# One core, a chunked scan beside dense products: the decay arguments and the causal mask move from ScalarE's bias and GpSimd to VectorE, and a group's two squares are added before the product that makes their mean

## What is computed

```python
# 32 heads of 64 channels in 8 groups of 4 heads; B, C: 128 states for each group; 256 tokens
a = dt * A                                   # per token and head, negative
cum = jnp.cumsum(a, axis=1)
decay = jnp.exp(jnp.where(causal, cum[i] - cum[j], -jnp.inf))      # for each head
cb = jnp.einsum('bign,bjgn->bgij', C, B)                           # for each group
y = jnp.einsum('bgij,bghij,bjghp->bighp', cb, decay, x * dt)
y = y + x * d_skip
g = y * silu(z)                                                    # gated
g = g * lax.rsqrt(jnp.mean(jnp.square(g), axis=-1) + EPS)          # over the 256 channels of a group
y_b = g * norm_w
mixed = sigmoid(gate_a) * (y_a @ w_branch_gm) + sigmoid(gate_b) * (y_b @ w_branch_ssm)
```

## Time and profile before

| what | value |
|---|---|
| three executions | 1598.72, 1596.85, 1600.15 us (median 1598.72) |
| the profiled execution, its own time | 1598.4 us |
| its span, first to last instruction | 1596.6 us |
| mean granted TensorE clock | 0.988 of 2.4 GHz |
| busy: TensorE, weight loads, VectorE, ScalarE, GpSimd | 97%, 94%, 62%, 49%, 12% of the span |
| scan, 237.5 to 375 us: busy TensorE, VectorE, ScalarE, GpSimd | 110.45, 64.69, 69.93, 68.48 us of 137.5 |

### The profile page before, as it was taken

One profiled execution on the slowest core, in us unless ns is written; L12 is line 12 of the kernel. 1 busy time (PEld: TensorE's weight loads), 2 busy tenths in 40 slices (PEclk: granted clock), 3 DMA queues, 4 the chain that ended last, 5 costly groups with the idle time before them and its releaser, 6 DMA issues.

```text
span 1596.6 us, 30154 instructions
## 1 busy us (share of the span) xinstructions
PE 1541.6 (97%) x12471; PEld 1501.9 (94%) x12471; DVE 994.3 (62%) x1275; ACT 775.5 (49%) x1021; POOL 198.5 (12%) x186
## 2 busy tenths in 40 slices
PE   7999997879999999999999999999999999999997
PEld 5999997768999999999999899999999999899997
DVE  5887994445676555655465775555755558765545
ACT  3555565554465534544354554443544435554433
POOL 0300004553100010000012011001300013030001
PEclk9999999989999999999999999999999999999999
DMA  8976864433545544555545335555455553455550
GB/s 317 370 286 230 293 237 155 155 119 127 210 166 184 185 170 173 185 184 184 185 147 197 132 110 208 184 184 185 158 185 184 184 185 133 159 185 184 184 185 27
DMA packets 43497, 296.00 MB, mean 185 GB/s; under 512 B 5147, under 2 KB 7323, under 8 KB 8844
## 3 DMA queue, kind: packets, MB, share of 16 engines
q1 hardware_dynamic: 41244, 284.44, 49.3%
q0 software_dynamic: 2160, 10.22, 1.8%
HBM read 291.44 MB, written 3.19 MB: 185 GB/s over the span
## 4 chain that ended last, share of the span: by engine, by line
PE 87%; DVE 7%; ACT 3%; issue 1%; DMA 1%; POOL 0%; ACTq 0%; SPq 0%; DVEq 0%; POOLq 0%
PE banks L654 20%; PE banks L657 20%; PE banks L656 20%; PE banks L782 6%; PE banks L785 6%; PE banks L784 6%; DVE w_lo L1676 2%; ACT w_hi L1215 1%; DVE XS L1824 1%; PE banks L671 1%; PE banks L666 1%; PE banks L668 1%; DVE H L1832 1%; DMA rows<-cum_rows 1%; PE banks L813 0%
## 5 line engine op out<-in xcount | busy, mean ns | idle before, releaser
L1676 DVE TENSOR_TENSOR w_lo<-raw,w_hi 128x1024 fp32r<-128x1024 f32 x490 | 620.5, 1275 | 478.0 <-ACT w_hi L1215 472.8
L1215 ACT ACTIVATE w_hi<-raw 128x1024 fp32r<-128x1024 f32 x490 | 515.3, 1057 | 563.4 <-PE banks L657 405.1
L654 PE MATMUL banks<-H,w_lo 128*128 128x256 f32 x1696 | 477.7, 282 | 2.9 <-DVE w_lo L1676 1.9
L656 PE MATMUL banks<-H,w_hi 128*128 128x256 f32 x1696 | 477.2, 281 | 0.0
L657 PE MATMUL banks<-H,w_hi 128*128 128x256 f32 x1696 | 477.2, 281 | 0.0
L654 PEld LDWEIGHTS banks<-H,w_lo 128*128 128x128 f32 x1696 | 319.2, 188 | 3.7 <-DVE w_lo L1676 2.5
L656 PEld LDWEIGHTS banks<-H,w_hi 128*128 128x128 f32 x1696 | 319.2, 188 | 0.0
L657 PEld LDWEIGHTS banks<-H,w_hi 128*128 128x128 f32 x1696 | 319.2, 188 | 0.0
L656 PE MATMUL banks<-HH,w_hi 128*128 128x256 f32 x960 | 270.1, 281 | 0.0
L657 PE MATMUL banks<-HH,w_hi 128*128 128x256 f32 x960 | 270.1, 281 | 0.0
L654 PE MATMUL banks<-HH,w_lo 128*128 128x256 f32 x960 | 270.1, 281 | 0.0
(11 more groups left out here) (293 smaller groups left out, 1896.9 us busy)
## 6 DMA issues: line engine op xcount, KB each, us to landing
raw<-in_panels SPq DMA_DIRECT2D x269, 1024.0 KB, 4.8
rows<-cum_rows POOLq DMA_DIRECT2D x16, 384.0 KB, 3.9
bias_rows<-rev POOLq DMA_DIRECT2D x1, 2048.0 KB, 15.3
XS<-in_x_t SPq DMA_DIRECT2D x1, 1024.0 KB, 7.2
near<-bias_rows POOLq DMA_DIRECT2D x8, 128.0 KB, 3.6
out_t<-XS SPq DMA_DIRECT2D x4, 256.0 KB, 2.6
ws<-in_ws_t POOLq DMA_DIRECT2D x1, 512.0 KB, 8.7
cols<-in_cols SPq DMA_DIRECT2D x1, 180.0 KB, 2.4
```

Source lines behind the costliest of these rows:

```text
L654: pe.matmul(acc, w_lo[:, panel_slot, at:at + P], operand[:, kk, 0, :], start=starts and c == chunks[0], stop=False)
L656: pe.matmul(acc, w_hi[:, panel_slot, at:at + P], operand[:, kk, 1, :], start=False, stop=False)
L1215: act.activation(w_hi[:, sl, w], raw[:, r, w], ACT.Copy).then_inc(panel_hi, 1)
L1676: vec.tensor_tensor(w_lo[:, sl, w], raw[:, r, w], w_hi[:, sl, w], ALU.subtract).then_inc(panel_lo, 1)
```

## The change

- The decay argument is made by VectorE: `decay_args` adds -cum to the rows and takes the minimum with 0, four operations in place for each step (256, 128, 256, 128 columns), one step ahead; it now holds the wait for the rows' DMA. ScalarE takes one exponential of 768 columns without a bias.
- GpSimd no longer masks the rows. A constant 0/1 matrix `causal` is made once, and the scores are copied out of PSUM by VectorE times that matrix (`causal_scores`) instead of by ScalarE.
- The scores go to bank 6, no longer shared with the variances; the outputs alternate between banks 5 and 7.
- `squares_added` (VectorE) adds a group's two squares; `group_sums` is one product instead of two, and stands in even steps.
- The variance stands in odd steps, the roots of four groups at step 11, `y_normed`, `y_hi` and `y_lo` one step later; the sums, variances and roots of groups 6 and 7 lie in the first three panels of branch_ssm.
- `never` goes; `keep_busy` multiplies by the identity.

```diff
@@ new names
+        causal = part[:, :, :].rearrange("p a t -> p (a t)")[:, 0:3 * P]
...
+        def output_bank(n):
+            return 5 + 2 * (n % 2)
@@ GpSimd
-            def rows_causal(n):
-                pool.wait_ge(rows_landed[n % ROW_SLOTS], 16 * (n // ROW_SLOTS) + 16)
-                for r in range(2):
-                    diagonal = rows[:, n % ROW_SLOTS, 3 * P * r:3 * P * r + T].rearrange("p (a i) -> p a i", a=2)
-                    pool.affine_select(out=diagonal, in_=diagonal, compare_op=ALU.is_ge, fill=MASKED, base=0,
-                                       pattern=[[0, 2], [1, P]], channel_multiplier=-1).then_inc(S["rows_masked"], 1)
             pool.wait_ge(S["cum_copied"], 1)
             pool.dma_start(cum_rows, cum_row[:, :]).then_inc(S["cum_stored"], 16)
             pool.wait_ge(S["cum_stored"], 16)
             for n in range(ROW_SLOTS):
                 rows_in(n)
-            rows_causal(0)
+            pool.wait_ge(S["mod_turned"], len(MOD_ORDER))
+            pool.memset(causal, 1.0).then_inc(S["causal_clear"], 1)
+            pool.wait_ge(S["causal_clear"], 1)
+            diagonal = causal.rearrange("p (a i) -> p a i", i=P)[:, 0:3:2, :]
+            pool.affine_select(out=diagonal, in_=diagonal, compare_op=ALU.is_ge, fill=0.0, base=0,
+                               pattern=[[0, 2], [1, P]], channel_multiplier=-1).then_inc(S["causal_set"], 1)
             for n in range(PAIRS):
-                if n + 1 < PAIRS:
-                    rows_causal(n + 1)
                 if n >= 2:
                     gating(n - 2)
-                pool.wait_ge(S["exp_done"], 4 * (n + 1))
+                pool.wait_ge(S["exp_done"], n + 1)
                 if n + ROW_SLOTS < PAIRS:
                     rows_in(n + ROW_SLOTS)
                 pool.wait_ge(S["cb_copied"], n // 2 + 1)
                 two = decay(n).rearrange("p (r i) -> p r i", r=2)
                 pool.tensor_tensor(two, two, cb[:, n // 2 % 2, :].unsqueeze(1).to_broadcast([P, 2, 3 * P]),
                                    ALU.mult).then_inc(S["m_done"], 1)
-                if n >= 12:
-                    y_lo(n - 12)
+                if n >= 13:
+                    y_lo(n - 13)
             gating(PAIRS - 2)
             gating(PAIRS - 1)
-            for g in range(4, SSM_GROUPS):
+            for g in range(3, SSM_GROUPS):
@@ TensorE
-                pe.matmul(banks[0:32, 6, P:2 * P], a_v[:, 0, :], tri[:, :], start=True, stop=True)
-                second = banks[0:32, 6, 0:3 * P].rearrange("q (a i) -> q a i", a=3)[:, 0:3:2, :]
+                pe.matmul(banks[0:32, 6, 0:P], a_v[:, 0, :], tri[:, :], start=True, stop=True)
+                second = banks[0:32, 6, P:3 * P].rearrange("q (a i) -> q a i", a=2)
...
-                    pe.matmul(banks[:, bank, 0:T], ident_r[:, :], never[:, :].unsqueeze(1).to_broadcast([P, 2, P]),
+                    pe.matmul(banks[:, bank, 0:T], ident_r[:, :], ident_r[:, :].unsqueeze(1).to_broadcast([P, 2, P]),
...
-                if g >= 2:
-                    pe.wait_ge(S["y_var"], g - 1)
-                pe.matmul(banks[:, 3, 0:T], B[:, g, 0:P], C[:, g, :], start=True, stop=True)
-                pe.matmul(banks[:, 3, T:3 * P], B[:, g, P:T], C[:, g, P:T], start=True, stop=True)\
+                pe.matmul(banks[:, 6, 0:T], B[:, g, 0:P], C[:, g, :], start=True, stop=True)
+                pe.matmul(banks[:, 6, T:3 * P], B[:, g, P:T], C[:, g, P:T], start=True, stop=True)\
                     .then_inc(S["cb_done"], 1)
                 if g:
                     pe.wait_ge(S["xdt_done"], 2 * g)
...
                 g = n // 2
                 pe.wait_ge(S["m_done"], n + 1)
                 pe.wait_ge(S["xdt_done"], 2 * (g + 1))
-                if n:
-                    pe.wait_ge(S["y_skip"], n)
+                if n >= 2:
+                    pe.wait_ge(S["y_skip"], n - 1)
                 m_of = decay(n)
                 for r in range(2):
-                    to = banks[HP * r:HP * r + HP, 7, 0:T]
+                    to = banks[HP * r:HP * r + HP, output_bank(n), 0:T]
                     cut = slice((n % 2 * 2 + r) * HP, (n % 2 * 2 + r + 1) * HP)
                     pe.matmul(to, xdt(g, 0)[:, cut], m_of[:, r * 3 * P:r * 3 * P + T], start=True, stop=False)
                     last = pe.matmul(to[:, P:T], xdt(g, 1)[:, cut], m_of[:, r * 3 * P + T:(r + 1) * 3 * P],
...
                 last.then_inc(S["y_done"], 1)
             def group_sums(g):
-                pe.wait_ge(S["y_sq"], 2 * (g + 1))
+                pe.wait_ge(S["y_added"], g + 1)
                 if g:
                     pe.wait_ge(S["y_var"], g)
-                for m in range(2):
-                    last = pe.matmul(banks[:, 3, 0:T], gmean_w[:, :], sq[:, 2 * (g % 2) + m, :],
-                                     start=m == 0, stop=m == 1)
-                last.then_inc(S["y_sums"], 1)
+                pe.matmul(banks[:, 3, 0:T], gmean_w[:, :], sq[:, 2 * (g % 2), :], start=True, stop=True)\
+                    .then_inc(S["y_sums"], 1)
...
-                if n % 2 and n >= 3:
-                    pe.wait_ge(S["cb_copied"], n // 2 + 1)
-                    group_sums((n - 3) // 2)
+                if n % 2 == 0 and n >= 4:
+                    group_sums((n - 4) // 2)
                 if n:
                     head_outputs(n - 1)
             head_outputs(PAIRS - 1)
...
                 for half in range(2):
                     pe.wait_ge(S["y_lo"], 2 * p + half + 1)
                     plan_half(q, half, YB)
-                if q == AT["branch_ssm", 0, 0]:
-                    group_sums(SSM_GROUPS - 1)
+                n = q - AT["branch_ssm", 0, 0]
+                if n == 0:
+                    pe.wait_ge(S["y_skip"], PAIRS - 1)
+                if n < 2:
+                    group_sums(SSM_GROUPS - 2 + n)
@@ ScalarE
-            def cb_copy(g):
-                act.wait_ge(S["cb_done"], g + 1)
-                if g >= 2:
-                    act.wait_ge(S["m_done"], 2 * (g - 1))
-                act.activation(cb[:, g % 2, :], banks[:, 3, 0:3 * P], ACT.Copy).then_inc(S["cb_copied"], 1)
             def decays(n):
-                act.wait_ge(S["rows_masked"], 2 * (n + 1))
+                act.wait_ge(S["decay_args"], 4 * (n + 1))
                 if n < 2:
                     act.wait_ge(S["silu_done"], SSM_GROUPS - 1 + n)
                 if n >= 2:
                     act.wait_ge(S["y_done"], n - 1)
-                for r in range(2):
-                    h = 2 * n + r
-                    for t, (at, size, row) in enumerate(((0, T, P), (T, P, 0))):
-                        row += 3 * P * r
-                        act.activation(decay(n)[:, 3 * P * r + at:3 * P * r + at + size],
-                                       rows[:, n % ROW_SLOTS, row:row + size], ACT.Exp,
-                                       bias=dtv[:, 4, t, h:h + 1]).then_inc(S["exp_done"], 1)
+                act.activation(decay(n), rows[:, n % ROW_SLOTS, :], ACT.Exp).then_inc(S["exp_done"], 1)
...
-                if n % 2 == 0:
-                    cb_copy(n // 2)
                 if n >= 2:
                     y_square(n - 2)
                 for q, half in fill_halves(n):
...
-                if n == 10:
+                if n == 11:
                     y_roots(0, 4)
-                if n == 12:
-                    act.wait_ge(half_used, 2 * AT["gate_b", 1, 1] + 2)
-                if n >= 12:
-                    y_hi(n - 12)
+                if n >= 13:
+                    y_hi(n - 13)
+            y_hi(3)
             y_square(PAIRS - 2)
+            y_square(PAIRS - 1)
             y_roots(4, 2)
-            y_roots(6, 1)
-            y_square(PAIRS - 1)
             for q in range(AT["branch_ssm", 0, 0], len(DENSE)):
                 name, g, p = DENSE[q]
                 n = q - AT["branch_ssm", 0, 0]
...
-                if n == 1:
-                    y_roots(7, 1)
+                if n in (1, 2):
+                    y_roots(5 + n, 1)
@@ VectorE
-            vec.wait_ge(S["consts_ready"], 7)
-            vec.tensor_scalar(never[:, :], tri[:, :], -1.0, -MASKED, ALU.add, ALU.mult).then_inc(S["never_set"], 1)
...
+            def decay_args(n):
+                vec.wait_ge(rows_landed[n % ROW_SLOTS], 16 * (n // ROW_SLOTS) + 16)
+                for r in range(2):
+                    h = 2 * n + r
+                    for t, (at, size) in enumerate(((0, T), (T, P))):
+                        args = rows[:, n % ROW_SLOTS, 3 * P * r + at:3 * P * r + at + size]
+                        vec.tensor_scalar(args, args, ncum[:, t, h:h + 1], 0.0, ALU.add, ALU.min)\
+                            .then_inc(S["decay_args"], 1)
+            def causal_scores(g):
+                vec.wait_ge(S["cb_done"], g + 1)
+                if g >= 2:
+                    vec.wait_ge(S["m_done"], 2 * (g - 1))
+                vec.tensor_tensor(cb[:, g % 2, :], banks[:, 6, 0:3 * P], causal, ALU.mult).then_inc(S["cb_copied"], 1)
```

(31 more changed lines are left out.)

10 lines of the change are left out of this document (3 added, 7 removed).

## The result

The changed kernel takes **1571.86 us** (median of 4 runs, 1571.28 to 1572.43), the kernel before on the same chip 1598.81 us (1596.85 to 1600.15). The ratio is 0.9832, with a 95% interval of [0.9815, 0.9849]: faster by 1.7%, some 27 us. The profiled execution took 1572.09 us (span 1570.4, mean clock 0.992), 26.3 us less than that of before.

A forecast was written before the change was run, and what follows sets the result against it. TensorE's stops in the scan were the time to win, with VectorE, held up by GpSimd, setting the pace from the third group. Start -11, groups 2 to 5 -11.3, last two -3: -25.3 from 1598.4 gives 1573 us, range 1557 to 1588.

The forecast's parts named there:

- Start, -11: Scan start: third group's scores begin at 261.7 us instead of 272.7, 11 us sooner.
- from there TensorE's list has no wait: Scan start: from about 249.5 us TensorE works without a stop until the third group's scores at 261.7.
- Groups 2 to 5, 12.9 us each, -11.3: Scan: four groups at VectorE's pace take 51.6 us instead of 62.9.
- The exclusion, "in full": Scan: GpSimd's two products a group block VectorE for their whole 3.66 us, bringing VectorE to 13.1 us a group.
- TensorE's need, 11.8 us a group: Scan: TensorE without stops needs 12.3 us a group, 11.8 after one product of `group_sums` goes.
- rival A: Scan: TensorE alone is the bound, groups 2 to 7 take 11.8 us each, 1557 us in all; chance 0.20.
- Last two groups, -3: Scan end: the last two groups take 36 to 37 us instead of 39.4.
- Together 34.8: Last two groups: VectorE's need of 23.6 us plus GpSimd's products and three `y_lo`, 11.2 us.
- The roots, "covered by the slack": Step 11 of the scan: the roots' table load and two ScalarE activations are covered by the rounding's slack.
- branch_ssm, 0: branch_ssm takes as long as before: first `y_lo` in time, no panel waits; change 0 us.
- B: Scan: waiting for added squares replaces the variance wait; only the start's 11 us are won, 1587 us; chance 0.21.
- C: Scan: VectorE inherits the wait for the rows' DMA, 18 us a group, 6 us slower, 1605 us; chance 0.05.

The follow-up runs named there:

- late square: ScalarE's square put behind the step's roundings and tanh evictions: 1570.6 us on the changed kernel, 1561.55 us on the version with product on VectorE.
- product on VectorE: Changed kernel with the product of decay and scores moved from GpSimd to VectorE: 1566.53 us, ratio 0.9797.

## Why the prediction was right, and which of its terms were not

The forecast was 1573 us within 1557 to 1588, and 1571.86 came out. The mechanism held in the main: the stops go, and VectorE is full from the third group on, as budgeted. But TensorE's own need is as large, so that in the changed kernel VectorE's pace costs little (0.7 us in groups 2 to 5); it shows only where TensorE comes earlier. And that the sum came so close, -25.3 against -26.3, is luck in part: the start gave 4.9 us less than its term, the groups behind it 2.2 and 5.3 more, branch_ssm 1.6 less, and the misses cancel.

- **Start, -11; measured -6.1.** The step that failed is "from there TensorE's list has no wait". The first part held: the exponentials of step 0 start at 246.35, and the first `head_outputs` at 249.95 was foreseen as "about 249.5". But gate_a's first eviction stands on ScalarE behind the square of step 0, whose chain runs through VectorE's skip, which was late, and GpSimd. That cost 2.55 us of stop and a spell at 1.2 GHz. The spell is not bound to that stop: with two products for the mean, the same code up to here, it came earlier, and the start gave 7.8 us instead of 6.1. With the square out of the way the third scores began at 262.98, against the 261.7 foreseen (the pieces listed add up to 261.55); 0.66 us of that is what is left of the stop.
- **Groups 2 to 5, 12.9 us each, -11.3; measured 12.35, -13.5.** The step is not VectorE's need but where it begins to count. The need was sized well: where VectorE was full throughout and TensorE early (the changed kernel with a late square) four groups took 50.8 us from 263.0 to 313.8, that is 12.7 each, and the forecast's own clock has them end at 313.3. In the changed kernel TensorE came 3.6 us later, which let VectorE catch up, so that 49.4 us were enough. The two terms are tied: part of what the start lost, the groups did not have to wait (2.2 of 4.9 us).
- **The exclusion, "in full".** For `decay_args` and `squares_added` beside a product it held: 3.48 instead of 1.00 us, 2.46 instead of 0.41. The Trainium skill ("SBUF — State Buffer", "Who interferes with whom") says that VectorE in a mode with two ports, which tensor_scalar can enter, and GpSimd shut each other out for whole instructions, and that a VectorE operation with two SBUF inputs contends with a GpSimd operation that reads SBUF; the trace agrees for both rows. The experiment that shows its price is the move of the product: one operation more on VectorE, 2.1 us less busy time in a group.
- **TensorE's need, 11.8 us a group; measured 12.07,** within 0.01 in sixteen groups of six kernels. One half panel and one `head_outputs` take 3.85 us (256.45 to 260.30 with the product on VectorE and the late square) where 2.85 and 0.81 were added up. The sum of pieces missed some 0.2 us between them. For rival A this would have been 0.27 us in six groups, 1.6 us.
- **Last two groups, -3; measured -8.3.** "Together 34.8" added all of GpSimd's work to VectorE's, three `y_lo` included. The first of them does hold VectorE up: four `decay_args` take 4.72 us beside a gating, a product and this `y_lo`. The second gives way: two splits take their undisturbed 2.35 us, and `y_lo` takes 3.45 instead of 1.3. The third begins at 346.48, as these groups end (timelines of VectorE and GpSimd):

```profile
328.37 4.72 DVE L2035 TENSOR_SCALAR rows<-rows,dtv 128x256 f32<-128x256 f32 x4
331.26 1.29 POOL L567 TENSOR_TENSOR YB<-xbc,YB 128x512 fp32r<-128x512 f32 x1
...
339.12 2.35 DVE L1655 TENSOR_TENSOR w_lo<-raw,w_hi 128x1024 fp32r<-128x1024 f32 x2
339.16 3.45 POOL L567 TENSOR_TENSOR YB<-xbc,YB 128x512 fp32r<-128x512 f32 x1 [1.17 <-ACT YB L1471]
```

  VectorE's busy time in those two groups is 12.8 + 16.4 = 29.2 us, not 34.8. Two `y_lo` at 1.3 us account for 2.6 of the 5.6 us; the rest was not taken apart. The wait for the last product was foreseen, and its stop measured 2.62 us.
- **The roots, "covered by the slack".** Right for the changed kernel and poorly weighed as a gain: the 17.25 us group without this move, among groups of 13.0, points to some 4 us of the -13.5 for moving them a step later, off the step of a `group_sums`. This is an estimate from one timeline.
- **branch_ssm, 0; measured +1.6.** No panel of it waits, but it starts behind the stop of 2.62 us and runs at a clock of 0.96.
- **Rivals.** B (the variance's place taken by another wait) does not occur, with one stop of 2.47 us before `group_sums`, in the last group. C needs VectorE to wait for the rows; it never does. Their landing takes 4.1 us in the median against 3.9, so a delay of these DMAs by VectorE's operations is not to be seen.

Where the 26.3 us come from can be put together from the issue of `near`: 14.1 from the scores' bank and its wait alone, 18.9 with the gating ahead of the mask, and the other 7.4 from the rest (one exponential for four, the copy of the scores off ScalarE, the masks gone, the new order of sums and variance, the second output bank, the roots a step later). That last part was not divided by runs.

The best versions, product on VectorE and late square, with the last step as it was or with skip, product and norm in this order, take 1561.6 us, 0.978 of before, and beat both kernels.

## What to carry to other kernels

When work moves between VectorE and GpSimd, budget the two as one engine for operations of the kinds measured here (operands in SBUF): such an operation costs its time on the engine that does it and as much on the other one if that has such work too. The faster engine can win by taking more, as here with 0.95 us for 1.83. Find the chain behind every bank that TensorE reuses, not only the one that the change touches; here a square with no hurry stood ahead of an eviction on which all waited. And a gain at one place is only kept if the next bound has slack: one edit won 5 us at the start and nothing at the end of the scan, until another tie was cut.

## What was not expected of the hardware

- Which of two engines gives way is not fixed. Against a product, VectorE's `decay_args` and addition of squares stretched (3.48 and 2.46 us) and the product did not (1.83 and 1.86); against two back-to-back splits GpSimd's `y_lo` stretched (3.45) and they did not. That the one already running keeps its time fits the splits, which began 0.04 us ahead, but not the addition: in the four groups from 266.6 its record begins 0.3 us ahead of the product's (282.91 and 283.22), inside GpSimd's issue of the rows' DMA, and it is the addition that stretches. Beside such an issue without a product it takes 0.42 us (at 267.92, product on VectorE), so the issue alone does not hold it. What decides is open.
- After stops of 2.62 and 2.46 us at the scan's end the next 45 us ran at 0.96 and 0.97, after stops of 1.80 and 0.59 us at 1.00. At the start the length of the stop alone does not tell: after 2.31 us (two products for the mean) the clock fell to 1.2 GHz within 2 us, after 2.30 us (the changed kernel) and 2.93 us (four exponentials, at 251.18) it did not, and it fell in those two only behind the next stop, of 2.55 and 2.21 us.
- In some profiled executions a long stretch of dense products goes 1% slower, with no wait and a recorded clock of 1.00: 252 or 253 products in 30 us, where 255 are the rule. It lasts some 150 us or more and costs 1.9 to 2.2 us. It was seen in five of the thirteen, at different places behind the scan, in one of them twice (the gating ahead of the mask, where the two make up its 4.0 us). Two windows, of the late square on the changed kernel and of the changed kernel:

```profile
1420.00:1450.00 30.00, 30.00 (x252) 30.00 (x251) 15.69 (x16) 13.32 (x16) 0.00 (x0) 1.00 0.50 175
```

```profile
1420.00:1450.00 30.00, 30.00 (x255) 30.00 (x254) 15.85 (x15) 13.32 (x15) 0.00 (x0) 1.00 0.53 196
```

  It is why small differences are read here from the scan's own end; they too are not safe below some 2 us, as the two starts of the same code show.
